# Scattering a pair's rows in two groups of four jobs in place of three groups

## The reference, cut to what matters

```
def hierarchical_moe(h, w_group, w_router, w1, w3, w2):
...
    gates = g_gate * jax.nn.softmax(top_vals, axis=-1)
    expert_id = grp[:, None] * EXPERTS_PER_GROUP + top_idx
...
    def expert_block(args):
        toks, e = args
        xb = t_pad[toks]
        return (jax.nn.silu(xb @ w1[e]) * (xb @ w3[e])) @ w2[e]
...
    y = jax.ops.segment_sum(y_slots, slot_tok, num_segments=N + 1)[:N]
    return y.astype(h.dtype).reshape(B, S, D)
...
        x = x + hierarchical_moe(rms_norm(x, norm_moe_w[l]), w_group[l], w_router[l],
                                 w_exp_gate[l], w_exp_up[l], w_exp_down[l])
```

## Time and profile before

| | |
|---|---|
| three runs | 1982.76, 1979.86, 1982.32 us; median 1982.32 us |
| profiled execution | 1977.34 us |
| its span, first to last instruction | 1975.6 us |
| TensorE matmul, busy share of the span | 94% |
| VectorE, ScalarE, GpSimd | 41%, 33%, 28% |
| mean granted TensorE clock | 0.982 |
| DMA | 313.40 MB, mean 159 GB/s |

### The profile page before, as it was taken

The page is one execution under the profiler, slowest core; times in us unless marked ns, Lnnn a source line. Parts: engine busy times, 40 slices in busy tenths (PEclk is TensorE's granted clock), DMA queues, the critical chain, the costliest instruction groups (busy, mean ns, idle before and its releaser), DMA issues. The chain is left out here.

```text
span 1975.6 us, 28971 instructions
## 1 busy us (share of the span) xinstructions
PE 1863.8 (94%) x11709; PEld 1371.4 (69%) x11709; DVE 817.6 (41%) x1645; ACT 657.5 (33%) x1376; POOL 545.4 (28%) x416
## 2 busy tenths in 40 slices
PE   6999979998999999996999998999969999999997
PEld 4789868887888666675878875987864444444443
DVE  4466465234322455535423246333253343243333
ACT  4542233332224455444344256344232111101110
POOL 2342233524553444256145221353210000000000
PEclk9999999999999999998999999999989999999999
DMA  5230112213113311153133221333618999999994
GB/s 162 65 90 25 44 52 75 78 47 122 54 56 96 96 33 44 34 184 121 43 104 124 66 70 40 86 98 101 262 44 316 414 413 416 418 419 417 419 420 179
DMA packets 132681, 313.40 MB, mean 159 GB/s; under 512 B 15280, under 2 KB 102080, under 8 KB 107968
## 3 DMA queue, kind: packets, MB, share of 16 engines
q1 hardware_dynamic: 132544, 311.49, 42.5%
HBM read 309.37 MB, written 2.10 MB: 158 GB/s over the span
## 5 line engine op out<-in xcount | busy, mean ns | idle before, releaser
L321 POOL TENSOR_TENSOR unit_low<-unit_ring,unit_high 128x512 fp32r<-128x512 f32 x332 | 438.4, 1345 | 780.1 <-ACT unit_high L314 780.0
L358 PE MATMUL dense<-hT,unit_high 128*128 128x512 f32 x560 | 229.6, 410 | 3.6 <-POOL unit_low L321 1.8
L359 PE MATMUL dense<-hT,unit_high 128*128 128x512 f32 x560 | 220.3, 393 | 0.0
L360 PE MATMUL dense<-hT,unit_low 128*128 128x512 f32 x560 | 220.2, 393 | 0.0
L314 ACT CAST unit_high<-unit_ring 128x512 fp32r<-128x512 f32 x332 | 186.2, 619 | 60.3 <-PE dense L360 30.9
L451 PE MATMUL dense<-unit_high,hT 128*128 128x256 f32 x704 | 203.2, 289 | 0.7 <-POOL unit_low L321 0.5
L453 PE MATMUL dense<-unit_high,hT 128*128 128x256 f32 x704 | 199.2, 283 | 0.0
L452 PE MATMUL dense<-unit_low,hT 128*128 128x256 f32 x704 | 199.1, 283 | 0.0
L451 PEld LDWEIGHTS dense<-unit_high,hT 128*128 128x128 f32 x704 | 134.9, 192 | 8.1 <-issue 2.6
L452 PEld LDWEIGHTS dense<-unit_low,hT 128*128 128x128 f32 x704 | 134.9, 192 | 0.6 <-issue 0.5
L453 PEld LDWEIGHTS dense<-unit_high,hT 128*128 128x128 f32 x704 | 134.8, 191 | 0.0
(11 more groups left out here) (598 smaller groups left out, 3516.3 us busy)
## 6 DMA issues: line engine op xcount, KB each, us to landing
expert_ring<-w_exp_gate SPq DMA_DIRECT2D x64, 1024.0 KB, 9.5
expert_ring<-w_exp_up SPq DMA_DIRECT2D x64, 1024.0 KB, 10.4
expert_ring<-w_exp_down SPq DMA_DIRECT2D x64, 1024.0 KB, 9.1
unit_ring<-w_in SPq DMA_DIRECT2D x55, 1024.0 KB, 5.2
unit_ring<-w_mkv SPq DMA_DIRECT2D x8, 1024.0 KB, 5.4
unit_ring<-w_br SPq DMA_DIRECT2D x14, 512.0 KB, 6.3
x<-x SPq DMA_DIRECT2D x8, 512.0 KB, 5.7
w_out_raw<-w_out SPq DMA_DIRECT2D x4, 1024.0 KB, 8.2
```

The source lines that it names most:

```text
L321: nc.gpsimd.tensor_tensor(low[:, at:at + 512], raw[:, at:at + 512], high[:, at:at + 512], ALU.subtract).then_inc(*self.split.up())
L358: nc.tensor.matmul(out, high[:, k, c], rh, start=(k == 0), stop=False)
L359: nc.tensor.matmul(out, high[:, k, c], rl, start=False, stop=False)
L360: last = nc.tensor.matmul(out, low[:, k, c], rh, start=False, stop=(k == kd - 1))
```

## The change

One line changes in TensorE's list. The tuple says which scatter jobs follow each of the four expands. Before: jobs 0 and 1 behind the first, 2 to 4 behind the second, 5 to 7 behind the third. After: jobs 0 to 3 behind the first, 4 to 7 behind the third, none behind the second.

```
@@ -4353,7 +4353,7 @@
                 gather(pe, 0, i)
             for p in range(PAIRS):
                 g, q = p // 2, p % 2
-                for i, rows in enumerate(((0, 1), (2, 3, 4), (5, 6, 7), ())):
+                for i, rows in enumerate(((0, 1, 2, 3), (), (4, 5, 6, 7), ())):
                     expand(pe, p, i)
                     if p == 0:
                         spread(pe, i)
```

## The result

The changed kernel takes 2016.93 us (median of four runs, 2016.47 to 2017.93), the kernel before 1982.44 us (four runs). The ratio is 1.0178, 95% interval 1.016 to 1.0195: 34.5 us slower. The forecast was 2010.8 us in a range of 2001 to 2018 us.

A forecast was written before the change was run, and what follows sets the result against it. TensorE's order was taken to bound the stage. Saving -5.3, first-group waits +25.5, second group +1.5 and clock +6.8 sum to +28.5 us, taking 1982.32 us to 2010.8 us, range 2001 to 2018 us.

The forecast's parts named there:

- The case with the best chance: Waits as summed, with the granted clock falling behind two to five of the long ones: 2007 to 2013 us, chance 0.50.
- the long waits: Six TensorE waits at the first group's fourth job: 3.4 us in pairs 6, 8, 10, 12; 3.1 us in 2 and 4.
- TensorE's order bounds the stage: In the mixture-of-experts stage TensorE never waits for weights, so whatever it waits for is added whole.
- Saving of 0.35 us a pair: One scatter group fewer saves 0.20 us, products back to back 0.15 us; 5.3 us over 15 pairs.
- The wait at the fourth job: First group's fourth job needs the first job's bank, freed by VectorE's late first addition; 25.5 us over all pairs.
- The second group, 0.1 us: Second group's fourth job finds its bank free just in time; 0.1 us taken in each of 15 pairs, 1.5 us.
- Sum without the clock: Saving, first-group waits and second-group cost together, leaving out the 6.8 us for the clock.
- The clock, 6.8 us: TensorE's granted clock may fall to half behind long waits, costing 1.7 us each; bounds 0 and 10.2 us.
- I take four of six: Clock loss counted behind four of the six longest waits, 6.8 us; nothing for pair 3's shorter wait, bound 1.7 us.
- The case in which every long wait costs: Rival: the clock falls behind all six long waits, 2014.2 us, with pair 3 too 2015.9 us; chance 0.23.
- The other rivals: Fourth job doesn't wait: 1977.0 us, chance 0.04; transfers set the pace: 1982.3 us, 0.04; clock holds: 2004.0 us, 0.17.

The follow-up runs named there:

- e1: Changed kernel with both groups of four scatter jobs one product later, behind the second gate and first up product; 1977.81 us, ratio 0.9989 to the kernel before.
- e7: Scatter groups of 3, 3 and 2 behind the first, third and fourth product in pairs 1 to 13, against the kernel before; 1977.5 us, ratio 0.9979.
- e4: Changed kernel with VectorE's token picks of the next group put behind the first four additions; 1985.57 us, ratio 1.0025 to the kernel before.
- e5: Changed kernel with all VectorE picks, next group's tokens and the pair's, behind the first four additions; 1979.99 us, ratio 0.9998 to the kernel before.
- e6: Changed kernel with groups of 3 and 5 jobs at the same places, the fourth job in the second group; 1981.25 us, ratio 0.9998 to the kernel before.
- e3: Changed kernel with unread extra products filling TensorE's wait before the first group's fourth job in pairs 2, 3, 4, 6, 8, 10, 12; 2005.24 us.
- e2: Changed kernel with three groups of 4, 2 and 2 jobs, keeping only the early fourth job; 2018.31 us, ratio 1.0194 to the kernel before.

## Why the prediction was right, point by point

The measured 2016.93 us lies within the range, 6.1 us above the forecast. The case with the best chance, the clock falling at two to five of the long waits (0.50, 2007 to 2013 us), did not come; the range held because its upper end, 2018 us, took in the clock at every wait. The waits were right as summed; how often the clock falls was a guess, and it was too low.

- **TensorE's order bounds the stage**: right. Each wait was added whole, and the next pair gave nothing back. The weights' landing (5.0 to 11.0 us) and a DMA rate that went from 419 to 386 GB/s in a long pair (pair 8, from 1744.25 to 1778.99 us) show the transfers following.
- **Saving of 0.35 us a pair**: right. e1 gives 0.12 + 2 x 0.11 = 0.34 us, e7 0.35 us.
- **The wait at the fourth job**: right in place, cause and size, 3.28 and 0.32 us in pairs 6 and 5 as forecast, 3.02 us in pair 2 (forecast 3.03), and 0.74 us from the start of the addition to the job. e4 and e5 show that VectorE's picks ahead of the addition are the cause, e6 that it is this one job.
- **The second group, 0.1 us**: right, 0.11 us (0.01 us late, 0.10 us for weights not loaded ahead).
- **Sum without the clock**: forecast 28.5 - 6.8 = 21.7 us; e3 has 21.9 us in the stretch.
- **The clock, 6.8 us**: the mechanism right, the size too small. The step that was off is "I take four of six", with nothing for pair 3. It fell at all seven, which makes 11.9 us at 1.7 us each; measured are 12.3 us, with 2.8 us in pair 2. This is nearly all of the difference between 28.5 and 34.2 us. The Trainium skill's page "TensorE: Matmul & The Clock Gate", section "HAM oscillation — how this bites in real kernels", has a kernel throttled anew in every round, behind waits of some 3 to 5 us. The waits here are 1.98 to 3.14 us; the changed kernel agrees with it at seven of seven, e2 at five of seven. The case in which every long wait costs was given 0.23 and 2014.2 to 2015.9 us; it is the one that came, and on top of it pair 2 paid nearly twice, which no case had.

The trace before had rows that spoke for this and that the prediction did not use: a wait of 3.20 us near the start, in sparser work but the nearest in size to the long ones, with the clock at half for the three microseconds behind it, and one of 5.38 us, inside which the clock fell at 488.6 us and stayed at half until 495.4 us, 6.8 us, as in pair 2.

```profile
20.91 6.39 PE L2218 MATMUL dense<-hT,w_small_split 128*56 128x512 f32 x20 [3.20 <-DVE hT L2370]
...
22.00:23.00 1.00, 1.00 (x4) 0.44 (x3) 0.00 (x0) 0.98 (x3) 1.00 (x2) 0.50 1.00 332
...
491.79 2.04 PE L1710 MATMUL core<-state,ssd_CT 128*128 128x256 f32 x4 [5.38 <-DVE yT L1376]
```

The other rivals fell: job 3 does wait, TensorE never waits for a weight, and the clock did not hold.

What stays open is what decides whether the clock falls at a given wait, and when. It fell behind the wait of 2.37 us in pair 0 in all ten profiles, and at 20 of the 22 waits of 1.98 us and more at a fourth job; e2 held at two, in pairs 2 and 4, where the changed kernel, with the same waits and the same work just before them, fell. The length of the wait alone doesn't decide it; that its place in time does is a guess, which no run here tested.

## What to carry to other kernels

With n banks in turn, n jobs in a row are free and the next one waits for the first reader; before a group is made larger than n (three here), look in the timeline for where the reader of its first job stands in its own list, not for how fast it is on average (VectorE was busy 12.42 of the 30.04 us of a pair here). A wait of 2 us or more on TensorE in the middle of dense work should be priced at itself and the clock loss behind it, here 1.4 to 2.8 us in the changed kernel and nothing to 3.0 us in e2, and that price may come due every time. And a saving from fewer switches between kinds of jobs is best taken where the reader has had its time, as in e7.

## What the runs showed of the hardware

The granted clock fell at idle times of 1.98 us (pair 3 of the changed kernel) as well as 3.13 us, and stayed at half for 3.4 us, or for 6.8 us where it fell 0.6 to 1.0 us before the wait was over (pair 2 of the changed kernel in both profiles, pair 8 of e2). It held at 2.87 and 2.83 us (pairs 2 and 4 of e2). Twelve products that nobody reads, 2.91 us in all, inside a wait of 3.3 us kept it at full (e3). The matmul pair of a scatter job released late takes 0.10 us longer, 0.34 against 0.24 us from the first matmul to the second; its weight load starts with the first matmul (1661.22 us in pair 5) and not ahead of it. Going from the fp32 products to a group of fp32r scatter matmuls and back costs 0.35 us in all (e7), going from that group to the gather's matmuls nothing that shows.
